# Reordered waits, loads, PSUM banks and small steps at the start of an fp32 transformer kernel

## The reference

```python
cond = jax.nn.silu(c)
mod = (cond @ ada_w[i] + ada_b[i]).reshape(B, N_MOD, D)
h = rms_norm(x, norm_mix[i]) * (1 + scale1) + shift1
...
proj = h @ w_in
q_lat = proj[..., :Q_LORA]
kv_lat = proj[..., Q_LORA:Q_LORA + KV_LORA]
k_rope = rope(proj[..., Q_LORA + KV_LORA:], pos)
q = (rms_norm(q_lat, g_qa) @ w_qb).reshape(B, S, MLA_HEADS, MLA_QK)
kv = (rms_norm(kv_lat, g_kva) @ w_kvb).reshape(B, S, MLA_HEADS, MLA_NOPE + MLA_V)
```

## Time and profile before

| | us |
|---|---|
| runs | 2077.68, 2077.98, 2083.40 |
| median | 2077.98 |
| the profiled execution, its own time | 2083.4 |
| its span, first to last instruction | 2081.6 |
| PE busy | 2005.9 (96%) |
| DVE busy | 1407.8 (68%) |
| ACT busy | 1121.3 (54%) |

### The profile page before, as it was taken

One profiled execution on the slowest core, in us unless ns is written; L12 is line 12 of the kernel. 1 busy time (PEld: TensorE's weight loads), 2 busy tenths in 40 slices (PEclk: granted clock), 3 DMA queues, 4 the chain that ended last, 5 costly groups with the idle time before them and its releaser, 6 DMA issues.

```text
span 2081.6 us, 35033 instructions
## 1 busy us (share of the span) xinstructions
PE 2005.9 (96%) x14340; PEld 1856.8 (89%) x14340; DVE 1407.8 (68%) x2510; ACT 1121.3 (54%) x1854; POOL 302.9 (15%) x328
## 2 busy tenths in 40 slices
PE   8999998999999989998899989999999999999997
PEld 5898998999888879998789889999999998888886
DVE  6877766767776657646755457999997765555554
ACT  5855534225666545435554444457767764444444
POOL 0010010000000000000000000008885960000000
PEclk9999999999999999999999999999999999999999
DMA  9565786336444327665334344554444445555553
GB/s 348 171 204 187 250 282 210 112 118 208 162 132 146 128 85 235 186 183 184 120 122 142 122 142 158 182 179 155 151 151 162 141 144 185 189 186 188 190 185 121
DMA packets 97743, 356.26 MB, mean 171 GB/s; under 512 B 11104, under 2 KB 11232, under 8 KB 97200
## 3 DMA queue, kind: packets, MB, share of 16 engines
q1 hardware_dynamic: 84240, 305.04, 44.3%
q0 software_dynamic: 12624, 48.08, 7.1%
q10 hardware_dynamic: 720, 0.91, 0.1%
HBM read 352.94 MB, written 1.05 MB: 170 GB/s over the span
## 4 chain that ended last, share of the span: by engine, by line
PE 90%; DVE 5%; ACT 3%; issue 1%; DMA 1%; ACTq 0%; DVEq 0%; POOL 0%
PE psum L573 23%; PE psum L574 23%; PE psum L575 23%; PE psum L566 18%; PE psum L580 2%; DVE wl L1930 1%; ACT wh L1338 1%; ACT work L1326 0%; DMA araw<-in_ada_w 0%; DVE C L1910 0%; DMA con<-in_con 0%; DVE mix_sq L1910 0%; ACT L1326 0%; DVE mlp_sq L1910 0%; DVE araw L1913 0%
## 5 line engine op out<-in xcount | busy, mean ns | idle before, releaser
L1930 DVE TENSOR_TENSOR wl<-raw,wh 128x1024 fp32r<-128x1024 f32 (+1 forms) x566 | 687.6, 1219 | 438.9 <-ACT wh L1338 438.2
L1338 ACT ACTIVATE wh<-raw 128x1024 fp32r<-128x1024 f32 (+1 forms) x566 | 593.9, 1050 | 485.6 <-PE psum L575 443.7
L573 PE MATMUL psum<-peer_hh,wh 128*128 128x256 f32 x1152 | 331.8, 288 | 4.2 <-DVE peer_hl L1902 4.0
L575 PE MATMUL psum<-peer_hh,wl 128*128 128x256 f32 x1152 | 325.9, 283 | 0.0
L574 PE MATMUL psum<-peer_hl,wh 128*128 128x256 f32 x1152 | 325.3, 282 | 0.0
L573 PEld LDWEIGHTS psum<-peer_hh,wh 128*128 128x128 f32 x1152 | 218.4, 190 | 5.5 <-issue 4.4
L574 PEld LDWEIGHTS psum<-peer_hl,wh 128*128 128x128 f32 x1152 | 218.3, 190 | 0.0
L575 PEld LDWEIGHTS psum<-peer_hh,wl 128*128 128x128 f32 x1152 | 217.0, 188 | 0.0
L573 PE MATMUL psum<-wh,csh 128*128 128x512 f32 x512 | 202.9, 396 | 0.0
L575 PE MATMUL psum<-wh,csl 128*128 128x512 f32 x512 | 202.7, 396 | 0.0
L574 PE MATMUL psum<-wl,csh 128*128 128x512 f32 x512 | 202.7, 396 | 0.0
(11 more groups left out here) (453 smaller groups left out, 4751.2 us busy)
## 6 DMA issues: line engine op xcount, KB each, us to landing
raw<-in_mlp_w SPq DMA_DIRECT2D x128, 512.0 KB, 4.3
raw<-in_eu SPq DMA_DIRECT2D x128, 512.0 KB, 3.5
raw<-in_ev SPq DMA_DIRECT2D x128, 512.0 KB, 3.4
araw<-in_ada_w POOLq DMA_DIRECT2D x76, 512.0 KB, 4.9
raw<-in_dil_qk SPq DMA_DIRECT2D x48, 512.0 KB, 3.8
raw<-in_dil_v SPq DMA_DIRECT2D x24, 512.0 KB, 3.5
raw<-in_w_in SPq DMA_DIRECT2D x16, 512.0 KB, 3.5
raw<-in_w_query SPq DMA_DIRECT2D x16, 512.0 KB, 3.5
```

The source lines that it names most:

```text
L573: e.matmul(o, l[0], r[0], start=start, stop=False, skip_group_check=loose)
L575: i = e.matmul(o, l[1], r[0], start=False, stop=stop, skip_group_check=loose)
L1338: e.activation(b.wh[v % NSPLIT][:, 0:cols], b.raw[v % NRAW][:, 0:cols], ACT.Copy).then_inc(S.hi, 1)
L1930: e.tensor_tensor(b.wl[v % NSPLIT][:, 0:cols], b.raw[v % NRAW][:, 0:cols], b.wh[v % NSPLIT][:, 0:cols].bitcast(F32), ALU.subtract).then_in ...
```

## The change

It reorders work in all programs, and removes or adds no arithmetic.

- ACT's queue: the order of the five loads becomes `c_col`, `posI`, `con`, `cond`, `vec`. ACT waits for `con` and `vec` before its half of the squares, no longer after them.
- DVE: its half of the squares moves from the very start behind the angles and behind the wait for `vec`.
- PE: waits for `vec` as well as `con` before its first instruction.
- SP: the modulation pieces for j = 4 to 7 are no longer all issued ahead of unit 4 of the weights. Now each pair of pieces is followed by one unit, and units 4 to 7 wait for DVE's splits as before.
- DVE: `products(6)` moves from j = 2 to j = 3 and `products(7)` from j = 3 to j = 4. Four small copies of sine and cosine move from behind the root of the latents to just behind the split of `unit("mla_w_in", 7)`, ahead of `lat_low`.
- ACT: `lat_root("kv")` moves behind three `lat_square`.
- PE: the bank of `kv(0)`'s first half is given back ahead of the banks of latents 3 and 4, no longer behind them.

```diff
--- before.py
+++ after.py
@@ -846,11 +846,10 @@
                         e.matmul(ps, l[1], r[0], start=False, stop=True).then_inc(S.unit, 1)
                     else:
                         mm(ps, l[1], r[0], False, k == 1, mark=("kvb", s, t) if k == 1 else None)
+                give("kvb", s, t, sem=S.act, key=("kvb", "v", s, t))
                 if (s, t) == (0, 0):
                     for c in (3, 4):
                         give("lat", c, sem=S.act, key=("lat", "square", c))
-                give("kvb", s, t, sem=S.act, key=("kvb", "v", s, t))
-                if (s, t) == (0, 0):
                     lat_sums("kv", (3, 4), 0)
                 if (s, t) == (0, 1):
                     k_rope()
@@ -942,6 +941,7 @@
             give("mla", "oT", c, sem=S.dve, key=("mla", "out", c))
 
         pe.wait_ge(S.c_con, 16)
+        pe.wait_ge(S.c_vec, 16)
         ps = take("n0", "sum")
         for k in (0, 1, 2, 3, 4, 5, 6, 7):
             if k < 4:
@@ -1429,21 +1429,21 @@
     def mla():
         m = b.mla
         e.dma_start(m.ccol, d["c_col"]).then_inc(S.c_col, 16)
+        e.dma_start(m.posI, d["pos_col"]).then_inc(S.pos_col, 16)
         e.dma_start(b.con, d["con"]).then_inc(S.c_con, 16)
-        e.dma_start(m.posI, d["pos_col"]).then_inc(S.pos_col, 16)
+        e.dma_start(b.cond, d["c_row"]).then_inc(S.c_cond, 16)
         e.dma_start(b.vec, d["vec"]).then_inc(S.c_vec, 16)
-        e.dma_start(b.cond, d["c_row"]).then_inc(S.c_cond, 16)
         ac.wait_ge(S.c_col, 16)
         act(m.ccol, m.ccol, ACT.Silu, mark="c col")
+        ac.wait_ge(S.c_con, 16)
+        ac.wait_ge(S.c_vec, 16)
         ac.wait_ge(S.c_x, 16)
         act(m.na[:, 0:1024], b.xT[:, 0:1024], ACT.Square, mark=("n0", "sq", 0))
         ac.wait_ge(S.c_cond, 16)
         act(b.cond, b.cond, ACT.Silu, mark=("cond",))
         ac.wait_ge(S.dve, at["angles"])
         act(m.trig, m.trig, ACT.Sin, mark=("trig",))
-        ac.wait_ge(S.c_con, 16)
         norm_tail("n0", 8, m.ntmp)
-        ac.wait_ge(S.c_vec, 16)
 
         def row(j):
             ac.wait_ge(S.pe, at["ada done", j])
@@ -1489,9 +1489,9 @@
         ac.wait_ge(S.unit, u + 1)
         lat_high(2)
         act(m.krT[0:32, :], bank("lat", 2)[0:32, 256:512], ACT.Copy, mark="k rope in")
-        lat_root("kv", 2, 256)
         for c in range(3):
             lat_square(c)
+        lat_root("kv", 2, 256)
 
         def head_root(key, z):
             h = m.hs[key]
@@ -2106,8 +2106,6 @@
 
     def mla():
         m = b.mla
-        ve.wait_ge(S.c_x, 16)
-        tt(m.na[:, 1024:2048], b.xT[:, 1024:2048], b.xT[:, 1024:2048], ALU.mult, mark=("n0", "sq", 1))
         ve.wait_ge(S.c_con, 16)
         ve.wait_ge(S.pos_col, 16)
         cp(m.pos, m.posI)
@@ -2133,6 +2131,8 @@
         ts(m.trig, m.trig, 3.1415925, -3.1415925, ALU.min, ALU.max, mark="angles")
         ve.wait_ge(S.c_vec, 16)
         stt(m.more, vc(b, "ada_b", 8, 8), 1.0, vc(b, "norm_mix", 0, 8), ALU.add, ALU.mult)
+        ve.wait_ge(S.c_x, 16)
+        tt(m.na[:, 1024:2048], b.xT[:, 1024:2048], b.xT[:, 1024:2048], ALU.mult, mark=("n0", "sq", 1))
 
         def product(c, slot):
             u = m.first[:, slot * UNIT:(slot + 1) * UNIT]
@@ -2175,10 +2175,16 @@
                 ada(j)
             ahead(j - AHEAD)
             low(j)
-            if j in (1, 2, 3):
-                products({1: 4, 2: 6, 3: 7}[j])
+            if j in (1, 3, 4):
+                products({1: 4, 3: 6, 4: 7}[j])
         unit("mla_w_in", 6)
+        ve.wait_ge(S.act, at["trig",])
+        sin, cos = m.trig[:, 0], m.trig[:, 1]
         unit("mla_w_in", 7)
+        for h in range(2):
+            cp(m.cs[:, :, 16 * h:16 * h + 16], cos)
+        ts(m.sn[:, :, 0:16], sin, -1.0, None, ALU.mult)
+        cp(m.sn[:, :, 16:32], sin)
 
         def lat_low(c):
             ve.wait_ge(S.act, at["k rope in"] if c == 2 else at["lat", "hi", c])
@@ -2202,12 +2208,6 @@
         for c in (3, 4, 0, 1, 2):
             lat_low(c)
         lat_root("kv", 2)
-        ve.wait_ge(S.act, at["trig",])
-        sin, cos = m.trig[:, 0], m.trig[:, 1]
-        for h in range(2):
-            cp(m.cs[:, :, 16 * h:16 * h + 16], cos)
-        ts(m.sn[:, :, 0:16], sin, -1.0, None, ALU.mult)
-        cp(m.sn[:, :, 16:32], sin)
 
         def kv(s):
             unit("mla_w_kvb", s)
@@ -2856,12 +2856,9 @@
         early(2 * j + 1)
     for j in range(3):
         weights(j)
-    early(6)
-    early(7)
-    weights(3)
-    for i in range(8, 16):
-        early(i)
-    for j in range(4, 8):
+    for j in range(3, 8):
+        early(2 * j)
+        early(2 * j + 1)
         weights(j)
     for u in range(8, len(PLAN)):
         weights(u)
```

## The result

The changed kernel takes 2091.35 us (median of six runs, 2090.43 to 2093.71), the kernel before 2079.57 (median of six, 2077.68 to 2083.40). The ratio is 1.0055 with a 95% interval of 1.0042 to 1.0068, so it is 11.4 us slower (8.7 to 14.1). The forecast had the direction, 8.4 us and 2086.4; the time lies 0.35 us above its range of 2082 to 2091. The profiled execution took 2092.84 us, with a span of 2091.1 against 2081.6.

The account below looks back on a forecast made before the run. PE was taken to bound the kernel, busy 96% of the span, with nothing to absorb a late start. Terms 6.85 + 0.44 + 1.15 = 8.4 us on the median 2077.98 gave 2086.4 us, range 2082 to 2091.

Parts of the forecast that it names:

- The five loads: ACT's small loads at the kernel's start: they land in order of issue, `vec` last at 13.8 us.
- S: The later start of PE at its first matmul: 14.9 instead of 8.05 us, so 6.85 us.
- DVE's half of the squares: At the start: ends near 15.2 us, needed only for PE's fifth call over 2 us later, so hidden.
- The copies: Sine and cosine copies on DVE, ahead of `latTl`: PE's `kv(0)` starts 0.44 us later, ends 0.4 to 0.5.
- The bank edit: At `k_rope`, PE waits for ACT to copy out the `kv` bank: 1.15 us, ends 1.0 to 1.5.
- Rival 2: First stage, 25 to 45 us: paced by loads, so PE catches up and only 2 to 5 us remain; chance 0.07.
- The loads of `first` behind unit 4: Pieces 10 to 15 trail the splits in `w_in`: zero cost to PE, upper end 2.5 us, no gain possible.
- The lead of DVE: At `w_in(5)`: `low(5)` ends at 40.0 against PE's 40.24, so 0.2 us are left of 1.6 in hand.
- rival 3: Pieces 12 to 15 come later, so PE waits at `w_in(4)` or `w_in(5)`; with 2.5 us, 10.9 in all; chance 0.2.
- The sums of squares: PE's first 16 instructions: cost 5.62 us as before, change taken as zero, ends -1.6 to +2.1 us.
- half speed after idleness: PE's first sums: the first seven took 0.48 us each, the other nine 0.25; PE will start so again.
- the queue run dry: When SP issues unit 4 and pieces 10, 11: the load queue is empty by some 23 us.

## Why the direction was right and the size too small

**What held.** The five loads land in order of issue: `vec` landed at 13.8 (10.7 us after its issue at 3.03), and S was 6.99 against 6.85. DVE's half of the squares was hidden, `cond` and the angles too. The copies cost 0.35 against 0.44. The bank edit stops PE at `k_rope`, 1.43 us when alone against 1.15 forecast; in the changed kernel only 0.60 of it shows. With the other edits in but no slow matmuls ahead it was 0.94 and 0.95, so the slow matmuls used up 0.35, and the other 0.5 went with the other edits. Rival 2 (absorbed by the first stage) is out: alone, the late start cost 7.1 us at `k_rope`, the sums taken off.

**Where it failed: "The loads of `first` behind unit 4".** I took zero with 2.5 us as upper end, and priced only PE's wait in `w_in`. That zero is the step that failed: in the changed kernel the moved loads and products cost 1.16 us in `w_in`, nearly 1.9 in the load of the `kv` weights and, through the wait, 1.22 of lower clock. Three things were wrong in it.
- The landing times. I had pieces 12 and 13 at 30.7 and 32.0 + S, that is 37.6 and 38.9; DVE could start on them at 40.70 and 41.98. PE was by then 7.95 us late, not 6.85, which explains 1.1. The other 2 us lie between the bytes and the landing: 2.26 MB up to piece 12 had been moved by some 38.7 us by the profile's rates, as I had counted, and the piece landed at 40.7; piece 13 shows about the same (2.79 MB by 39.9, landed at 41.98). I had put some 2 us ahead of the data and none behind, but SP issued unit 4 at 30.82 and data flowed from about 31.6. I did not test what the difference is. DVE waited 2.88 us for piece 12:

```profile
40.70 1.23 DVE L1913 CUSTOM_DVE_ANT_0 first<-first,cond 128x1024 f32<-128x1024 f32 x1 [2.88 <-DMA first<-in_ada_w]
```

- The lead of DVE. I had 0.2 us in hand at `w_in(5)`, with `low(5)` done at 40.0. That sum was wrong: two passes of 1.15 us more put its end from 38.66 to 40.96, and `w_in(5)` began at 40.24. With all pieces on time PE already waited 0.52 there. Late pieces added only 0.41 to that, since DVE had idled 2.48 us for ACT at the same place anyway. Together 0.93 of idle, 1.16 in the ledger. This is rival 3 and within its price, as far as `w_in` goes.
- What comes behind. Piece 15 releases POOL, and I named that only as something "for" rival 3. POOL's 2 MB then met the `kv` weights. The unit took 7.33 us, ACT waited 2.37 us for it, and `kv(0)` came 2.22 later, of it about 0.35 for the copies. No term of the sum had this queue in it.

**A term that was missing.** With the wait of 3.06 us PE's clock fell at `kv(0)`: 1.22 us up to the first sum of latents. I had priced waits by their length alone.

**A term that was mis-sized.** The sums of squares: 6.59 against 5.62, within the ends that I gave (-1.6 to +2.1) but taken as zero. Over the fourteen kernels it ranged from 5.42 to 6.73 us with no tie to the edits, so I take it as noise of one execution. My reason for the slower first matmuls, half speed after idleness, is not in the record of the granted clock, which reads 1.00 throughout the sums in both kernels; what makes them slow stays open.

**The base.** I set the shift on a median of three runs, 2077.98; with six it was 2079.57. That alone is 1.6 us, more than the 0.35 us by which the time left the range.

With the mechanisms that ran, the ledger is 6.99 + 0.96 + 1.16 + 2.22 + 1.22 + 0.81 = 13.4 us at `k_rope`, and the same at the end of the block. It adds up because it is read from one timeline. The parts measured alone do not quite: at `k_rope`, the sums taken off, the late start cost 7.1, the loads and products 5.0, the bank 1.4 and the copies with `lat_root` 0.2, 13.7 together against 12.4 in the kernel after. There the bank's wait is shorter, and so is the stretch of lower clock.

## What to carry to other kernels

When a load is moved, follow what its landing releases on every other queue, and ask whether that stream will meet another one where it has no time to spare; the piece that a kernel loads last is often what starts the next stream. When PE gets a new wait, its clock can fall (here with waits of 2.55 to 3.06 us, not with 0.85 and 1.19), so price the slower work behind it as well as the wait. And compare variants at a mark in the trace just behind the edited stage: here it separated parts of about 1 us, once the sums were taken off, where the times of whole runs of one kernel spread by 3 to 12. The mark nearest the edit (`k_rope`) was the sharpest.

## What the runs showed of the hardware that was not expected

- After idle times of 2.55 and 2.93 us PE first ran at full speed, fell to half 0.5 and 0.9 us later and stayed there past `k_rope` (from 50.8 to 57.6 and from 51.7 to 58.5). With 2.83 (the kernel after without the bank edit) and 3.06 us the clock fell 0.2 and 0.5 us before PE started again, and was back ahead of `k_rope` (from 57.1 to 60.5 and from 58.5 to 61.9). After 0.85 and 1.19 us it did not fall.
- With SP held at unit 4 the DMA engines stood empty from 24 to 31 us, after being full until then. The forecast had the queue run dry at some 23 us, but not how long. In the kernel before the same stretch had a DMA share of 1.03 and 408 GB/s. Now:

```profile
26.00:28.00 2.00, 2.00 (x11) 0.76 (x9) 1.65 (x2) 0.00 (x0) 0.00 (x0) 1.00 0.00 0
```

- A load of 1 KB (`posI`) at the second place of ACT's queue, ahead of `con`, set `con` back: it landed 8.2 us after issue with the new order against 6.9, was issued 0.5 later, and PE started 1.83 us later.
